# Four buffers for gathered rows in the routed experts of a decoder layer, and two steps moved

## The chip, the cores and the metric

The kernel runs on one core of a Trainium2 chip. The metric is the device time of one execution in microseconds, and the time of a kernel is the median over its runs.

## The reference

One decoder layer over 2048 tokens of width 1024, all in float32. A mixer (sliding window attention beside a gated recurrence) is followed by a layer norm; then comes a mixture of experts and a second layer norm. The change touches the mixture of experts and the end:

```python
h = _layernorm(ALPHA * h + mix, ln1_g[l], ln1_b[l])
# _moe: every token goes to 8 of 64 experts; the pairs are sorted by expert and cut into blocks of 128 rows
def body(acc, blk):
    toks, bw, e = blk                      # 128 token numbers, their weights, one expert
    xb = hp[toks]                          # gather
    yb = (jax.nn.silu(xb @ w_gate[e]) * (xb @ w_up[e])) @ w_down[e]
    return acc.at[toks].add(yb * bw[:, None]), None     # scatter with addition
...
shared = (jax.nn.silu(hf @ ws_gate) * (hf @ ws_up)) @ ws_down
h = _layernorm(ALPHA * h + acc + shared, ln2_g[l], ln2_b[l])
```

An expert has 1024 x 256 gate and up weights and 256 x 1024 down weights. In this input no expert has fewer than two blocks, as the order of the splits in the trace shows.

## The kernel before

The program has four stages, each a block in which every engine runs its own instruction stream: the mixer, the output projection with routing and placing, the routed experts (`experts`), and the shared expert of the last eight tiles with the second norm (`share_and_norm`).

**The split.** Float32 products are made on TensorE out of high and low parts. A raw tensor is copied to a high part by ScalarE (`ACT.Copy` into float32r), VectorE subtracts that from the raw one and gets the low part. So every weight and every activation costs a copy on ScalarE and a subtraction on VectorE. For an expert these are two halves of gate and up (`gu_hi`, `gu_lo`, split 0 and split 1) and the down weights (`d_hi`, `d_lo`, split 2).

**The experts' loop.** A turn is two steps (n = 0 and 1 in the code, with slot k = 0 and k = 1), one block of 128 rows each; the loop runs the number of turns that a table gives, here 81. A step of TensorE is: low part of gate and up for the next block, the down product `psY` of this block (12 matmuls), high part of gate and up for the block after, then the transposes of `H`. Slot 0's rows come as whole rows and TensorE transposes them (`psX`). Slot 1's rows come in four pieces and VectorE transposes them (`xF<-xg`, L2510 and L2512), in the step with k = 0.

**VectorE's step** in program order: `HT_lo` (L2589), the low part of the activations (`low_x`, L2518 or L2523), the row weights, `H` (L2565), with k = 0 the transposes of slot 1's rows (`turn_x`), split 0 of an expert whose first block is two blocks ahead, the copy of `psY`'s second half to `y` (L2602), split 1 of the same expert, and last split 2 (`d_lo`) if the next block is the first of its expert. TensorE's `psY` of the next step waits for `y`, and its fifth matmul for `HT_lo`. ScalarE makes `d_hi` at the end of the step before an expert's first block.

**GpSimd's step** in program order: wait for the index and the buffer, gather for the block four ahead (one indirect DMA for slot 0, four for slot 1), then wait for `y` and issue the scatter (L2406). There is one buffer for each slot's rows (`xg[0]`, `xg[1]`), so a gather can be asked for only when the transposes have read the block before.

**SyncE** loads the weights of the experts in order; the down weights of a buffer are loaded over when `dlo_s` says that split 2 has read them.

**The last stage.** SyncE issues the loads of the routed sums `acc` into `z`, in groups of three tiles (2g, 2g + 1 and 8 + g) for g below 4 and of one tile after that, with two loads of `hT_d` between, all without a wait. GpSimd adds the second sums to each tile by a DMA that adds (`add_second`, L2862), two groups ahead of the norm's arithmetic, which it issues behind them in the same stream. ScalarE's `squares(1)` waits for GpSimd's `mean(1)`, and TensorE's down product of the next tile waits for `high_HT`, which ScalarE has behind `squares`.

Of the kernel before, what the change touches and what calls it, by code (L numbers as in the profile page):

```python
# [6 lines left out]
P = 128  # L7
D = 1024
SEQ = 2048
TILES = SEQ // P  # L10
KC = D // P
# [21 lines left out]
QUADS = 4  # L33
# [10 lines left out]
AHEAD = 4  # L44
# [1628 lines left out]
def place_and_share(nc, ident, consts, place_in, mask, cum, dpf, dbf, table, n_turns, idx, pidx, tails_s, xg, gi, gi_s, x_in,  # L1673
# [10 lines left out]
    with ExitStack() as ctx:  # L1684
# [145 lines left out]
        @block.gpsimd  # L1830
        def _(pool):
            for k in range(2):
                pool.wait_ge(row_out[k], 32 * TILES // 2)
                pool.wait_ge(hT_out[k], 16 * TILES // 2)
                pool.wait_ge(kept_out[k], 16 * (TILES - EARLY) // 2)
            nc.gpsimd.memset(zeros[:], 0.0).then_inc(zeroed, 1)
            nc.clear_and_free_semaphores(spent)

            pool.wait_ge(pads_out, 48 + 16 * QUADS)
            for k in range(2):  # L1840
                pool.wait_ge(wt_out[k], 48 * TILES // 4)
            nc.gpsimd.memset(xg[1][:, :, PIECE:WIDE], 0.0).then_inc(tails_s, 1)
            pool.wait_ge(idx_s, 2)
            nc.gpsimd.tensor_copy(gi[0][:], idx[:, 0:1]).then_inc(gi_s, 1)
# [3 lines left out]
            nc.gpsimd.tensor_copy(gi[1][:], pidx[:, 0, :]).then_inc(gi_s, 1)  # L1848
            pool.wait_ge(gi_s, 2)
            gather_pieces(nc, hcut, xg[1], gi[1], x_in[1])  # L1850
# [348 lines left out]
def experts(nc, passed, w_gate, w_up, w_down, ident, htab, hcut, sums, table, n_turns, idx, pidx, tails_s, xg, gi, gi_s, x_in, acc_out, gu, guhi_s, gulo_s, wgu, wd, loaded, y, si, added,  # L2199
# [6 lines left out]
    with ExitStack() as ctx:  # L2206
# [21 lines left out]
        pairw = [sb(f"pairw{i}", [P, 1]) for i in range(2)]  # L2228
        psG = [ps(f"psG5_{i}", [P, 2 * FE]) for i in range(2)]
# [95 lines left out]
        def turns(eng, body):  # L2325

            nt = eng.value_load(n_turns[0:1, 0:1], min_val=0, max_val=BLOCKS // TURN)
            with eng.Fori(0, BLOCKS // TURN // BUNCH) as j:
                with eng.If(j * BUNCH < nt):
                    with eng.Fori(0, BUNCH) as q:  # L2330
                        i = j * BUNCH + q
                        with eng.If(i < nt):
                            body(i)
                        with eng.Else():
                            eng.sem_inc(passed, 1)
                with eng.Else():
                    eng.sem_inc(passed, 1)
            return nt
# [32 lines left out]
        def _(pool):  # L2371
            for k in range(2):
                if k == 0:
                    pool.wait_ge(turned[1], 1)
                    pool.wait_ge(pairw_s[0], 1)
                    nc.gpsimd.tensor_copy(gi[0][:], idx[:, 2:3]).then_inc(gi_s, 1)
                    pool.wait_ge(gi_s, 3)
                    gather_rows(nc, htab, xg[0], gi[0], x_in[0])
                else:
                    pool.wait_ge(odd_turned, 1)  # L2380
                    nc.gpsimd.tensor_copy(gi[1][:], pidx[:, 1, :]).then_inc(gi_s, 1)
                    pool.wait_ge(gi_s, 4)
                    gather_pieces(nc, hcut, xg[1], gi[1], x_in[1])
            nc.clear_and_free_semaphores(spent)
            for k in range(2):
                pool.wait_ge(acc_out[k], 16 * EARLY // 2)

            def body(i):
                for n, s, k in steps(i):


                    pool.wait_ge(next_gi_s, s.n + 1)
                    if k == 0:
                        pool.wait_ge(pairw_s[0], s.turn + 2)
                    carry_wait(pool, passed)
                    if k:
                        gather_pieces(nc, hcut, xg[1], gi[1], x_in[1])
                    else:
                        gather_rows(nc, htab, xg[0], gi[0], x_in[0])
                    s.wait(pool, si_s)  # L2400
                    for h in range(2):
# [5 lines left out]
                                                 in_=y[k][:], in_offset=None, compute_op=ALU.add).then_inc(added[k], 16)  # L2407

            nt = turns(pool, body)
            for k in range(2):  # L2410
                pool.wait_ge(x_in[k], (nt * (16 * TURN // 2) + 16 * AHEAD // 2) * (QUADS if k else 1))
# [3 lines left out]
        def _(act):  # L2415
# [11 lines left out]
            def gather_index(s, k):  # L2427
# [3 lines left out]
                if k:  # L2431
                    nc.scalar.activation(gi[1][:], pidx[:, bass.ds(s.turn + AHEAD // 2, 1), :].rearrange("p a g -> p (a g)"),
                                         ACT.Copy).then_inc(next_gi_s, 1)
                else:
                    nc.scalar.activation(gi[0][:], idx[:, bass.ds(s.n + AHEAD, 1)], ACT.Copy).then_inc(next_gi_s, 1)

# [48 lines left out]
            def body(i):  # L2485
                nexts = entries(act, i * TURN + 1, TURN + 1)
                for n, s, k in steps(i):
# [3 lines left out]
                    gather_index(s, k)  # L2491
# [10 lines left out]
        def _(dve):  # L2502
            def turn_x(nth):

                dve.wait_ge(x_in[1], nth * 16 * QUADS)
                if not (isinstance(nth, int) and nth == 1):
# [4 lines left out]
                                    xg[1][:, :, 0:FEATS].rearrange("p g (i c) -> p c g i", c=KC))  # L2511
                nc.vector.transpose(xF[:, KC, :].rearrange("p (g j) -> p g j", g=QUADS),  # L2512
                                    xg[1][:, :, FEATS:WIDE]).then_inc(odd_turned, 1)
# [33 lines left out]
            def pair_weight(entry, nth, slot):  # L2547
# [6 lines left out]
                dve.wait_ge(x_in[0], nth * 16)  # L2554
                carry_wait(dve, passed)
                nc.vector.tensor_copy(pairw[0][:], xg[0][:, bass.ds(entry.expert() + D, 1)]).then_inc(pairw_s[0], 1)
# [16 lines left out]
            pair_weight(block0, 1, 0)  # L2573
            dve.wait_ge(tails_s, 1)
            turn_x(1)
# [4 lines left out]
            when_first(dve, block0, lambda: split(block0, 2))  # L2580
# [3 lines left out]
            def body(i):  # L2584
                nexts = entries(dve, i * TURN + 1, TURN + 1)
                for n, s, k in steps(i):
# [6 lines left out]
                    if k == 0:  # L2593
                        pair_weight(nexts[n + 1], s.turn + 2, 0)
                        pair_weight(nexts[n], s.turn + 1, 1)
# [7 lines left out]
                    when_first(dve, nexts[n + 1], lambda: split(nexts[n + 1], 1))  # L2603
                    when_first(dve, nexts[n], lambda: split(nexts[n], 2))
# [4 lines left out]
        def _(pe):  # L2609

            def turn_x(nth):

                pe.wait_ge(x_in[0], nth * 16)
                carry_wait(pe, passed)
                rows = xg[0][:, 0:D].rearrange("p (q c) -> p c q", c=KC)
# [56 lines left out]
            turn_x(1)  # L2672
# [6 lines left out]
            turn_x(2)  # L2679

            def body(i):
                words = entries(pe, i * TURN, TURN + 2)
                for n, s, k in steps(i):
# [24 lines left out]
                    if k:  # L2708
                        turn_weights(s.turn + 2)
                        turn_x(s.turn + 3)  # L2710
# [12 lines left out]
def share_and_norm(nc, passed, ident, ln2_g, ln2_b, hT_d, acc, second, out, raw_gu, raw_d, shared_in, hT_in, n_turns, added):  # L2723
# [3 lines left out]
    with ExitStack() as ctx:  # L2727
# [90 lines left out]
        def _(sp):  # L2818
# [18 lines left out]
            for g in range(LATE):  # L2837
                for t in (2 * g, 2 * g + 1):
# [304 lines left out]
def decoder_layer(nc, x, w_in, conv_w, conv_b, w_rg, b_rg, w_ig, b_ig, lam, sinks, g_attn, g_lru, w_out,  # L3143
# [9 lines left out]
    with ExitStack() as ctx:  # L3153
# [77 lines left out]
        with ExitStack() as routing:  # L3231
# [26 lines left out]
            xg = [gathered.enter_context(nc.sbuf_tensor(f"xg{i}", shape, F, side="right"))  # L3258
                  for i, shape in enumerate(([P, ROW_W], [P, QUADS, WIDE]))]
            gi = [gathered.enter_context(nc.sbuf_tensor(f"gi{i}", [P, n], I32, side="right")) for i, n in enumerate((1, QUADS))]  # L3260
            pidx = gathered.enter_context(nc.sbuf_tensor("pidx", [P, WORDS // 2, QUADS], I32, side="right"))
            gathered.enter_context(nc.sbuf_tensor("gap_gu", [P, 8], F, side="right"))
            tails_s = gathered.enter_context(nc.semaphore("tails_s"))
            gi_s = gathered.enter_context(nc.semaphore("gi_s"))
            x_in = [gathered.enter_context(nc.semaphore(f"xg_in{i}")) for i in range(2)]
# [76 lines left out]
```

## Time and profile before

| | |
|---|---|
| median of 3 runs | 2506.89 us (2502.52 to 2510.63) |
| profiled execution, its own time | 2510.86 us |
| its span from the first to the last instruction | 2509.0 us |
| mean granted TensorE clock | 0.973 |
| TensorE busy | 2357.9 us (94%) |
| VectorE busy | 1758.6 us (70%) |
| ScalarE busy | 1179.1 us (47%) |
| GpSimd busy | 972.2 us (39%) |

The profiled execution's own time has 1.9 us around its span. The experts' loop lies between about 872 and 2386 us of the span, the last stage behind it. A busy engine is not an engine at its peak, and the idle time of an engine matters only where another one waits for it.

### The profile page before, as it was taken

The numbers are of one execution on the slowest core, as the hardware profiler recorded it, in microseconds if no ns is written. First come the engines' busy times: TensorE is split into PE (matmuls) and PEld (weight loads), VectorE is DVE, ScalarE is ACT, GpSimd is POOL, SyncE is SP. The second block draws the span as 40 slices with busy tenths as digits, with TensorE's granted clock in tenths as the row PEclk, the third lists the DMA queues.
The fourth block names the chain that finished last, engine by engine and source line by source line (L and its number), as shares of the span: only waits on it lengthen the run. The fifth ranks groups of instructions, "written<-read, shape, count | busy, mean of one in ns | idle before, by whom it ended". The sixth has DMA issues, their size and how long they took to land. (4 is left out here: it accounts for less than half of the span.)

```text
span 2509.0 us, 49346 instructions
## 1 busy us (share of the span) xinstructions
PE 2357.9 (94%) x11266; PEld 1904.2 (76%) x11268; DVE 1758.6 (70%) x2382; ACT 1179.1 (47%) x1863; POOL 972.2 (39%) x772
## 2 busy tenths in 40 slices
PE   8899999999998799999999999999999999999966
PEld 6576777678886677888778887787778888877855
DVE  6686767758878767667767677667766677767437
ACT  3525253532225545455554545545554546545334
POOL 0010100011110155554555555554655556555437
PEclk9999999979998899999999999999999999999988
DMA  6143434465655478878887878888888789887796
GB/s 252 76 168 122 137 116 141 136 222 196 216 206 208 167 240 269 248 220 271 254 269 232 260 232 247 272 261 257 255 241 249 226 240 300 274 247 229 180 248 202
DMA packets 165327, 551.13 MB, mean 220 GB/s; under 512 B 31344, under 2 KB 56080, under 8 KB 144784
## 3 DMA queue, kind: packets, MB, share of 16 engines
q1 hardware_dynamic: 109696, 355.03, 40.1%
q0 software_dynamic: 54960, 195.27, 31.0%
q8 instruction: 36, 0.59, 0.1%
q14 instruction: 27, 0.22, 0.0%
q10 hardware_dynamic: 608, 0.02, 0.0%
HBM read 394.99 MB, written 155.25 MB: 219 GB/s over the span
## 5 line engine op out<-in xcount | busy, mean ns | idle before, releaser
L2647 PE MATMUL psG<-gu_split,xT_hi 128*128 x2624 | 626.0, 391 | 3.4 <-ACT xT_hi L2421 1.9
L2647 PEld LDWEIGHTS psG<-gu_split,xT_hi 128*128 128x128 f32 x2624 | 494.9, 189 | 107.5 <-issue 4.1
L1669 POOL DMA_INDIRECT xg<-hcut,gi x332 | 376.6, 1134 | 144.0 <-issue 92.5
L2661 PE MATMUL psG<-gu_split,xT_lo 128*128 x1304 | 341.2, 403 | 0.0
L2526 DVE TENSOR_TENSOR gu_split<-raw_gu,gu_split (+1 forms) x127 | 289.4, 2279 | 69.2 <-ACT gu_split L2444 59.5
L2406 POOL DMA_INDIRECT acc<-y,si x81 | 170.4, 2104 | 413.1 <-DVE y L2602 376.5
L2661 PEld LDWEIGHTS psG<-gu_split,xT_lo 128*128 128x128 f32 x1304 | 233.1, 189 | 42.4
L2444 ACT ACTIVATE gu_split<-raw_gu x126 | 234.4, 1908 | 33.2 <-issue 16.6
L2510 DVE STREAM_TRANSPOSE xF<-xg 128x1024 f32<-128x1024 f32 x82 | 177.2, 2161 | 91.8 <-DMA xg<-hcut,gi 91.7
L2526 DVE TENSOR_TENSOR d_lo<-raw_d,d_hi (+1 forms) x64 | 146.6, 2291 | 123.9 <-ACT d_hi L2444 123.9
L2699 PE MATMUL psY<-d_hi,HT_lo 128*128 x648 | 204.3, 397 | 18.8 <-DVE HT_lo L2589 18.8
L2489 ACT ACTIVATE HT_hi<-psH 128x256 fp32r<-128x256 f32 x162 | 62.2, 384 | 335.0 <-PE psH L2668 335.0
L2699 PE MATMUL psY<-d_hi,HT_hi 128*128 x648 | 204.2, 396 | 16.2 <-DVE y L2602 11.6
L2406 POOL DMA_INDIRECT second<-y,si x81 | 193.9, 2394 | 35.6 <-issue 35.6
L2699 PE MATMUL psY<-d_lo,HT_hi 128*128 x648 | 200.8, 391 | 0.0
L2699 PEld LDWEIGHTS psY<-d_hi,HT_lo 128*128 128x128 f32 x648 | 119.2, 189 | 55.8 <-issue 33.1
L2699 PEld LDWEIGHTS psY<-d_hi,HT_hi 128*128 128x128 f32 x648 | 119.9, 188 | 51.8 <-issue 26.8
L2444 ACT ACTIVATE d_hi<-raw_d (+1 forms) x64 | 122.7, 1917 | 60.1 <-PE psY L2699 60.1
L2602 DVE COPY y<-psY 128x512 f32<-128x512 f32 x162 | 109.7, 677 | 51.6 <-PE psY L2699 51.6
L2699 PEld LDWEIGHTS psY<-d_lo,HT_hi 128*128 128x128 f32 x648 | 122.3, 189 | 26.6
L950 PE MATMUL psP<-xT_hi,wring 128*128 128x512 f32 x512 | 131.8, 407 | 11.2 <-ACT xT_hi L468 3.6
L418 POOL TENSOR_TENSOR OS<-QK 128x256 f32<-128x256 f32 x15 | 11.1, 739 | 317.6 <-ACT QK L560 317.6
(404 smaller groups left out, 4038.9 us busy)
## 6 DMA issues: line engine op xcount, KB each, us to landing
raw_gu<-in_w_gate_dram SPq DMA_DIRECT2D x64, 1024.0 KB, 5.2
raw_gu<-in_w_up_dram SPq DMA_DIRECT2D x64, 1024.0 KB
raw_d<-in_w_down_dram SPq DMA_DIRECT2D x64, 1024.0 KB
wring<-split_d SPq DMA_DIRECT2D x24, 1024.0 KB, 5.8
second<-blank SPq DMA_DIRECT2D x17, 512.0 KB, 6.8
split_d<-wring POOLq DMA_DIRECT2D x8, 1024.0 KB, 4.2
raw_d<-mixed SPq DMA_DIRECT2D x16, 512.0 KB, 5.3
xt<-in_x_dram SPq DMA_DIRECT2D x16, 512.0 KB, 5.7
```

The source lines that it names most:

```text
L418: nc.gpsimd.tensor_tensor(OS2[:], OSQ[:, 0:2, :], OSQ[:, 2:4, :], ALU.add).then_inc(os2_s, 1)
L950: m = nc.tensor.matmul(u.tile[:], w_[:, w, k, :], xT[x_][:, k, :], start=(n == 0), stop=(n == len(passes) - 1))
L1669: nc.gpsimd.indirect_dma_start(out=to[:, g, 0:PIECE], out_offset=None, in_=hcut.rearrange("r a w -> (r a) w"), in_offset=bass.IndirectOffs ...
L2406: nc.gpsimd.indirect_dma_start(out=sums[k], out_offset=bass.IndirectOffsetOnAxis(ap=si[k][:, 0:1], axis=0), in_=y[k][:], in_offset=None, c ...
L2444: nc.scalar.activation(dst, src, ACT.Copy).then_inc(done, 1)
L2489: nc.scalar.activation(HT_hi[:], psH[:, 0:FE].rearrange("p (a b) -> p a b", a=2), ACT.Copy).then_inc(HThi_s, 1)
L2510: nc.vector.transpose(xF[:, 0:KC, :].rearrange("p c (g j) -> p c g j", g=QUADS), xg[1][:, :, 0:FEATS].rearrange("p g (i c) -> p c g i", c=KC))
L2526: nc.vector.tensor_tensor(dst, src, hi, ALU.subtract).then_inc(dlo_s if n == 2 else gulo_s, 1)
L2602: nc.vector.tensor_copy(y[k][:, 512:], psY[:, 1, :]).then_inc(y_s[1], 1)
L2647: nc.tensor.matmul(psG[slot][:], xT_hi[slot][:, c, :], right[:, bass.ds(w, 1), c, :].rearrange("p a n -> p (a n)"), start=(n == 0 and c == ...
L2661: m = nc.tensor.matmul(psG[slot][:], xT_lo[slot][:, c, :], gu_hi[:, bass.ds(w, 1), c, :].rearrange("p a n -> p (a n)"), start=False, stop= ...
L2699: m = nc.tensor.matmul(psY[:, h, :], left[:, c, :], right[:, bass.ds(w, 1), c, h * 512:(h + 1) * 512].rearrange("p a n -> p (a n)"), start ...
```

## The change

- `xg` and `gi` get two buffers for each slot, `xg[k][side]`, and semaphores of their own. The loop's body is written out twice, for an even turn (side 0) and an odd turn (side 1), and the inner loop runs half as often. `AHEAD` goes from 4 to 6 blocks. Two more gathers stand ahead of the loop, with a second memset of the tail columns.
- GpSimd's step has the scatter first and the gather behind it.
- VectorE's split 2 leaves the end of the step before an expert's first block. It is made in the step of that first block, behind `turn_x` and ahead of split 0 and the copy of `y`.
- In the last stage SyncE waits, before the loads of group g (from 2 on), until the second sums of the last tile of group g - 2 have been added.
- A gap in the memory layout goes from 8 to 112 columns.

```diff
-AHEAD = 4
+AHEAD = 6
@@ turns
-                    with eng.Fori(0, BUNCH) as q:
-                        i = j * BUNCH + q
-                        with eng.If(i < nt):
-                            body(i)
-                        with eng.Else():
-                            eng.sem_inc(passed, 1)
+                    with eng.Fori(0, BUNCH // 2) as q:
+                        for side in range(2):
+                            i = j * BUNCH + q * 2 + side
+                            with eng.If(i < nt):
+                                body(i, side, j * (BUNCH // 2) + q)
+                            with eng.Else():
+                                eng.sem_inc(passed, 1)
@@ gpsimd, body
+                    s.wait(pool, si_s)
+                    for h in range(2):
+                        s.wait(pool, y_s[h])
+
+                    pool.wait_ge(added[k], s.turn * 16)
+                    carry_wait(pool, passed)
+                    nc.gpsimd.indirect_dma_start(out=sums[k], out_offset=..., in_=y[k][:], in_offset=None, compute_op=ALU.add).then_inc(added[k], 16)
                     pool.wait_ge(next_gi_s, s.n + 1)
                     if k == 0:
                         pool.wait_ge(pairw_s[0], s.turn + 2)
                     carry_wait(pool, passed)
+                    to = 1 - side
                     if k:
-                        gather_pieces(nc, hcut, xg[1], gi[1], x_in[1])
+                        gather_pieces(nc, hcut, xg[1][to], gi[1][to], x_in[1][to])
                     else:
-                        gather_rows(nc, htab, xg[0], gi[0], x_in[0])
-                    s.wait(pool, si_s)
-                    ...  (the wait for y and the scatter stood here)
@@ vector, ahead of the loop
             when_first(dve, block0, lambda: split(block0, 1))
-            when_first(dve, block0, lambda: split(block0, 2))
@@ vector, body
                     if k == 0:
-                        turn_x(s.turn + 2)
-                    when_first(dve, nexts[n + 1], lambda: split(nexts[n + 1], 0))
+                        turn_x(s.turn + 2, 1 - side, pair + 1 + side)
+                    when_first(dve, words[n], lambda: split(words[n], 2))
+                    when_first(dve, words[n + 2], lambda: split(words[n + 2], 0))
                     s.wait(dve, yps_s[1])
                     dve.wait_ge(added[k], s.turn * 16)
                     nc.vector.tensor_copy(y[k][:, 512:], psY[:, 1, :]).then_inc(y_s[1], 1)
-                    when_first(dve, nexts[n + 1], lambda: split(nexts[n + 1], 1))
-                    when_first(dve, nexts[n], lambda: split(nexts[n], 2))
+                    when_first(dve, words[n + 2], lambda: split(words[n + 2], 1))
@@ share_and_norm, sync
             for g in range(LATE):
+                if 2 <= g:
+                    sp.wait_ge(z_all[EARLY + g - 2], 16)
                 for t in (2 * g, 2 * g + 1):
                     if t < EARLY:
                         load_z(t)
```

Here `nexts` began one block later than `words` does, so `nexts[n]` is the same block as `words[n + 1]`.

## Rows read from the trace of the kernel before

**Rows 1.** Busy us: window, PE, PEld, DVE, ACT, POOL; PEclk, DMA share, GB/s.
```profile
872.00:2386.00 1514.00, 1476.99 (x6923) 1210.19 (x6924) 1052.15 (x1249) 765.63 (x1245) 818.49 (x573) 1.00 0.83 249
```
**Rows 2.** Waits of TensorE, 900 to 2380 us: total us, times, longest.
```profile
PE psY L2699 <- DVE HT_lo L2589: 18.8, 23, 0.9
PE psY L2699 <- DVE y L2602: 11.6, 13, 1.8
```
**Rows 3.** Busy time: twelve turns together, and two turns with late gathers.
```profile
1320.10:1534.30 214.20, 214.20 (x1017) 177.13 (x1017) 148.18 (x181) 107.53 (x181) 118.51 (x85) 1.00 0.83 243
1783.70:1824.70 41.00, 37.92 (x172) 30.29 (x172) 25.50 (x34) 17.77 (x30) 23.38 (x16) 0.96 0.92 265
```
**Rows 4.** Busy time in seven windows that hold 21 slow turns, their sum.
```profile
sum 420.10, PE 388.21 PEld 310.17 DVE 300.62 ACT 223.62 POOL 213.23; mean PE 55.46 PEld 44.31 DVE 42.95 ACT 31.95 POOL 30.46
```
**Rows 5.** Timeline of VectorE in one slow turn: start, us, idle before.
```profile
1239.50 2.29 DVE L2526 TENSOR_TENSOR d_lo<-raw_d,d_hi  x1 [2.44 <-ACT d_hi L2444]
...
1243.54 0.48 DVE L2565 SCALAR_TENSOR_TENSOR H<-psG,pairw,sg 128x256 f32<-128x256 f32 x1
1246.32 2.18 DVE L2510 STREAM_TRANSPOSE xF<-xg 128x1024 f32<-128x1024 f32 x1 [2.29 <-DMA xg<-hcut,gi]
...
1250.77 0.70 DVE L2602 COPY y<-psY 128x512 f32<-128x512 f32 x1
...
1253.56 0.44 DVE L2589 TENSOR_TENSOR HT_lo<-psH,HT_hi 128x256 fp32r<-128x256 f32 x1
```
**Rows 6.** Timeline of TensorE in the same turn.
```profile
1252.12 0.72 PE L2699 MATMUL psY<-d_hi,HT_hi 128*128 x2 [0.64 <-DVE y L2602]
...
1254.15 0.70 PE L2699 MATMUL psY<-d_hi,HT_lo 128*128 x2 [0.85 <-DVE HT_lo L2589]
```
**Rows 7.** A turn with splits 0 and 1 and no late gather: busy time.
```profile
1517.30:1535.30 18.00, 18.00 (x86) 14.73 (x85) 13.77 (x15) 10.66 (x16) 9.76 (x7) 1.00 0.66 189
```
**Rows 8.** Waits of VectorE, 900 to 2380 us.
```profile
DVE xF L2510 <- DMA xg<-hcut,gi: 89.6, 38, 5.7
DVE HT_lo L2589 <- ACT HT_hi L2489: 89.2, 36, 3.6
```
**Rows 9.** Timeline at the end of the loop: GpSimd's last two, TensorE's last matmul.
```profile
2384.88 0.95 POOL L1669 DMA_INDIRECT xg<-hcut,gi  x1 [0.30 <-issue]
2386.13 1.63 POOL L2406 DMA_INDIRECT second<-y,si  x1 [0.30 <-issue]
...
2393.15 0.79 PE L2713 MATMUL psG<-gu_split,xT_hi 128*128 128x512 f32 x1 [5.14 <-issue]
```
**Rows 10.** Timeline of the last stage on GpSimd.
```profile
2416.96 0.86 POOL L2862 DMA_DIRECT2D z<-second  x1 [3.19 <-DMA z<-acc]
...
2428.45 0.87 POOL L2862 DMA_DIRECT2D z<-second  x1 [2.98 <-DMA z<-acc]
2429.40 0.25 POOL L2894 TENSOR_SCALAR nmean<-total 128x1 f32<-128x1 f32 x1
...
2441.79 0.88 POOL L2862 DMA_DIRECT2D z<-second  x1 [1.01 <-DMA z<-acc]
```
**Rows 11.** Timeline of the last stage on VectorE and TensorE.
```profile
2416.96 1.22 DVE L3020 TENSOR_TENSOR z<-z,psY 128x1024 f32<-128x1024 f32 x1 [3.49 <-DMA z<-second]
...
2434.16 2.05 PE L3127 MATMUL psY<-s_d,HT_hi 128*128 128x512 f32 x4 [14.57 <-ACT HT_hi L2947]
```
**Rows 12.** DMA queues of the last stage: packets, MB, share of 16 engines.
```profile
q0 software_dynamic: 2784, 10.10, 41.0%
q1 hardware_dynamic: 4896, 17.83, 37.6%
```
**Rows 13.** All DMA queues that carried anything, 920 to 2380 us.
```profile
q0 software_dynamic: 49257, 170.73, 46.9%
q1 hardware_dynamic: 36525, 192.94, 36.6%
```
**Rows 14.** TensorE's first instruction in the experts' stage.
```profile
868.73 1.94 PE L2620 MATMUL psX<-ident,xg 128*128 128x128 f32 x8 [3.65 <-issue]
```

More of the change, by code:

```diff
@@ L2407, in body @@
                                                  in_=y[k][:], in_offset=None, compute_op=ALU.add).then_inc(added[k], 16)
+                    pool.wait_ge(next_gi_s, s.n + 1)
+                    if k == 0:
+                        pool.wait_ge(pairw_s[0], s.turn + 2)
+                    carry_wait(pool, passed)
+                    to = 1 - side
+                    if k:
+                        gather_pieces(nc, hcut, xg[1][to], gi[1][to], x_in[1][to])
+                    else:
+                        gather_rows(nc, htab, xg[0][to], gi[0][to], x_in[0][to])
             nt = turns(pool, body)
             for k in range(2):
-                pool.wait_ge(x_in[k], (nt * (16 * TURN // 2) + 16 * AHEAD // 2) * (QUADS if k else 1))
+                for side in range(2):
+                    pool.wait_ge(x_in[k][side], ((nt + AHEAD // TURN + 1 - side) >> 1) * 16 * (QUADS if k else 1))
             carry_wait(pool, passed)
@@ L2483, in _, with body @@
             when_first(act, block1, lambda: split_gate_up(block1, 1))
-            def body(i):
+            def body(i, side, pair):
                 nexts = entries(act, i * TURN + 1, TURN + 1)
@@ L2502, in _, with turn_x @@
         def _(dve):
-            def turn_x(nth):
-                dve.wait_ge(x_in[1], nth * 16 * QUADS)
+            def turn_x(nth, side, landed):
+                dve.wait_ge(x_in[1][side], landed * 16 * QUADS)
                 if not (isinstance(nth, int) and nth == 1):
@@ L2545, in split, with pair_weight @@
                 low(n, src, hi, lo)
-            def pair_weight(entry, nth, slot):
+            def pair_weight(entry, nth, slot, side=None):
                 if slot:
@@ L2572, in _ @@
                 dve.wait_ge(acc_out[k], 16 * EARLY // 2)
[L2573 to L2575 removed]
+            pair_weight(block0, 1, 0, 0)
+            dve.wait_ge(tails_s, 2)
+            turn_x(1, 0, 1)
             when_first(dve, block0, lambda: split(block0, 0))
@@ L2609, in _, with turn_x @@
         def _(pe):
-            def turn_x(nth):
-                pe.wait_ge(x_in[0], nth * 16)
+            def turn_x(nth, side, landed):
+                pe.wait_ge(x_in[0][side], landed * 16)
                 carry_wait(pe, passed)
-                rows = xg[0][:, 0:D].rearrange("p (q c) -> p c q", c=KC)
+                rows = xg[0][side][:, 0:D].rearrange("p (q c) -> p c q", c=KC)
                 for h in range(2):
@@ L2671, in _ @@
             block0, block1 = entries(pe, 0, 2)
-            turn_x(1)
+            turn_x(1, 0, 1)
             gate_up_high(1, 0, block0, 1)
@@ L2678, in _, with body @@
             turn_H(0)
-            turn_x(2)
-            def body(i):
+            turn_x(2, 1, 1)
+            def body(i, side, pair):
                 words = entries(pe, i * TURN, TURN + 2)
@@ L2709, in body @@
                         turn_weights(s.turn + 2)
-                        turn_x(s.turn + 3)
+                        turn_x(s.turn + 3, side, pair + 2)
             turns(pe, body)
```

72 lines of the change are left out of this document (34 added, 38 removed).

## The prediction, made before the changed kernel ran

> **What bounds the kernel now.** I read the busy time by stage first. The experts' loop has 1514 of the 2509 us, and TensorE is busy for 1476.99 of them, at the full granted clock [rows 1]. So the stage runs at TensorE's pace, and the change can only win back what TensorE loses there. The second view is what TensorE waits for: 18.8 us for VectorE's `HT_lo` and 11.6 us for VectorE's copy to `y` [rows 2]. Matmuls are pipelined and a short wait shows only in part, so the third view is the length of the turns, taken from the starts of the first `psY` matmul in the timeline. Twelve turns in a row without a stall take 214.2 us, 17.85 each, and TensorE is busy in all of it [rows 3]. Of the 80 turns that can be measured, 57 take 17.8 to 18.1 us, and 23 are longer. Of these, 21 have one and the same form and take 420.1 us together, 20.0 each [rows 4]. The other two follow each other and take 41.0 us [rows 3]. So stalls cost 21 x 2.15 + 5.3 = 50 us of the loop.
>
> The reader is to see what the 21 have in common. In VectorE's timeline of one of them `turn_x` starts 2.29 us late, because slot 1's gathered rows have not landed; split 0, the copy to `y`, split 1 and `HT_lo` stand behind it in that order [rows 5]. TensorE then waits 0.64 us for `y` and 0.85 us for `HT_lo` [rows 6]. All 21 have splits 0 and 1 in the step with k = 0 and a gather that is over 2 us late. A turn with these splits and no late gather takes 18.0 us [rows 7]. With a late gather and no such splits a turn takes 17.85, so nearly half of the 38 waits for the gather [rows 8] cost nothing. The length of a turn with these splits is about 17.6 us plus the wait for the gather: 19.67 us with the shortest, 2.04 us, and 20.65 with 3.07 us, in the same timelines.
>
> **The buffers and the order on GpSimd.** A second buffer for each slot lets the gather be asked for a whole turn, 17.85 us, earlier. The longest wait is 5.7 us [rows 8], so all of them go. GpSimd's work is the same; the scatter of slot 1 no longer stands behind four issues of 0.95 + 0.30 us [rows 9], and the gathers, now behind the scatter, have a turn to spare. I cost the new order at nothing; if that spare turn were gone, the cost would be the waits that are there now.
>
> **Split 2, a step later.** This is where the gain goes. For an expert whose first block is at slot 0, `d_lo` stood at the end of the step before, one with k = 1. VectorE did it there in idle time: it had waited 2.44 us for `d_hi` ahead of it [rows 5]. After the change the same subtraction stands in the step with k = 0, behind `turn_x` and ahead of split 0 and `y`, if this block is the first of its expert. Splits 0 and 1 stand there if the block two ahead is a first one. Both hold exactly for an expert of two blocks that begins at slot 0. The timeline shows `d_lo` at the end of the step before in all 21 slow turns: they are these experts. In the 15 turns with splits 0 and 1 and no late gather there was no `d_lo` in the step before. So in every one of the 21 the wait for the gather is taken out, and a subtraction of 2.29 us is put in its place. `H` can't come earlier to make up for it, since it follows at once on the silu that waits for TensorE. Instructions that follow each other without a wait overlap by about 0.08 us (`turn_x` begins 0.08 us before `H` ends in turns without a late gather), so the subtraction counts as a wait of 2.29 - 0.16 = 2.13 us. A slow turn becomes 17.6 + 2.13 = 19.7 us: 21 x (20.0 - 19.7) = 6 us, of which I take 5, as these waits may be shorter in other executions. Where the first block is at slot 1, `d_lo` moves to a step without `turn_x`: three subtractions and the copy are 3 x 2.2 + 0.6 = 7.2 us against the 9.4 us of such a step, and the idle time of up to 3.6 us that VectorE has ahead of `HT_lo` [rows 8] covers the rest. If that cover were gone, each of some ten such turns would be 1 to 2 us longer.
>
> The two other long turns had gathers 2.94 and 5.68 us late, with `d_lo` at the end of a step with k = 0. Both causes go: 41.0 - 2 x 17.85 = 5.3 us. But the profiled execution takes 2510.86 us, 4.0 above the median, and such an accident may be in it alone. I count 5 us against the profiled execution and 2 against the median.
>
> SyncE asks for the next down weights up to 7 us later, since `dlo_s` comes later, and for nothing else: gate and up of the next expert wait for splits that come behind. The weights are used two experts on; hidden.
>
> **The loop written twice.** The skipped turns behind the last one are 5.14 us of issue on TensorE [rows 9]; half as many back edges may save up to 1 us. I take nothing. At the end GpSimd's scatter comes first and the four pieces last: `y` is ready near 2384, so their issue ends at 2384 + 1.6 + 4 x 1.25 = 2391 us. They landed some 6 us behind the last issue in the slow turn [rows 5], with full queues; here I estimate 2 to 6. The stage then ends between 2393 and 2397, against 2393.9, the end of TensorE's last matmul [rows 9]: 0 to 3 us, of which I take 1.
>
> **Loads in groups.** `z<-acc` lands and `z<-second` is issued every 3.85 us: three times from 2416.96 to 2428.45 [rows 10]. The two queues share the engines by halves; the shares of this stage give 46 us for 34 half megabytes on the one, 1.4 each, and 50 us for 19 on the adding one, 2.6 each [rows 12]. Now the ninth load lands at 2428.45, GpSimd's mean stands behind it at 2429.40 [rows 10], ScalarE's squares behind that, and TensorE waits 14.57 us until 2434.16 [rows 11]. After the change the loads of group 2 are asked for when the third tile's second sums are in, at 2416.96 [rows 11], just when the sixth load has landed. The loading queue runs empty for some 2.5 us, the additions get ahead by one, and that costs the ninth load 2.6 us. Nothing wins it back: the twelfth load (2441.79) waits behind the same bytes, and the norm behind it runs at its own pace. From below 0, if the engines lose nothing; from above 4 us, if the next handover does it again. I take 3. The output's stores are issued later too, behind the last load, but the last store waits for the last tile as before.
>
> **The sum** against the profiled execution: -5 (slow turns), -5 (late gathers), +1 (end of the loop), +3 (loads), -6 in all: 2504.9. Against the median, with -2 for the second term: 2506.9 - 3 = 2503.9. In proportion to the profiled execution it would be 2500.9; I take 2502.
>
> **The rivals.** (1) The slow turns go altogether, since VectorE finds 2.1 us elsewhere. They would then take the 18.0 us of the turn without the wait [rows 7]: 21 x 2.0 = 42, and with 2 for the late gathers and 4 for the ends 2506.9 - 42 - 2 + 4 = 2467. For it: the subtraction leaves the end of the step before. Against it: VectorE was idle there [rows 5], and `H` waits for TensorE.
> (2) The loads in groups cost more than the loop gives back. Where a handover leaves both queues dry, each of the two that matter (groups 2 and 3) costs a pair of 3.85 us, and with 3 for the loop's end that is 11: 2506.9 + 11 - 4 = 2514. It decides from 7 us on. For it: the first handover falls on an empty queue [rows 11]; against it: additions are in flight at each.
> (3) The doubled body no longer stays in an engine's instruction memory. In the loop before only the two data queues carried anything [rows 13], so no instructions were fetched. Where TensorE enters new code it stands for 3.65 us [rows 14]; at 40 back edges that is 146 us, 2650. On VectorE the 3.6 us ahead of `HT_lo` [rows 8] would hide it. The Trainium skill (Runtime: NRT & Kernel Launch, Instruction fetch mechanics) says that a taken branch out of the window that an engine holds costs a fetch before execution goes on. The trace agrees so far that a body of one turn stays in; no run here shows two.
> (4) The gathers are as late as before, because contention and not the request sets their landing. Then slow turns have the wait and the subtraction: 21 x 2.1 = 44, 2551. Against it: no wait was over 5.7 us [rows 8], and a turn is three times that.
>
> **How the numbers follow.** A measurement of this kernel tells 0.3%, 7.5 us, from no change: faster is below 2499.4, slower above 2514.4. The forecast (2495 to 2509) has 0.6: 0.2 of it below 2499.4, 0.4 within. Rival 1 has 0.1, faster. Rival 2 (2508 to 2518) has 0.15: 0.06 within, 0.09 slower. Rival 3 has 0.06, slower. Rival 4 and mishaps not named have 0.09: 0.02 faster, 0.01 within, 0.06 slower. Faster 0.32, same 0.47, slower 0.21. The range leaves out rival 1, rival 3 and the far part of the rest: 2490 to 2514.
>
> **What the changed profile would show.** Right: VectorE's wait for the gather falls from 89.6 us to under 5; in the same 21 turns its order is `turn_x`, `d_lo`, split 0, `y`, split 1, `HT_lo` without a gap; TensorE's waits for `y` and `HT_lo` stay above 20 us together, and these turns take 19.6 to 19.8. The ninth addition of the last stage lies 2 to 4 us later behind the stage's start, and TensorE's long wait with it. Wrong: turns of 18.1 us where three splits meet (rival 1), instruction fetches in the loop (rival 3), or a last stage that gets shorter.

## The result: slower, and where the time went

| | before | after |
|---|---|---|
| median us | 2506.25 (2502.52 to 2510.63) | 2544.47 (2539.73 to 2547.38) |
| profiled execution, its span | 2510.86, 2509.0 | 2547.38, 2545.6 |

The ratio is 1.015, with a 95% interval of 1.0127 to 1.0173: 38 us or 1.5% slower, where 2502 with a range of 2490 to 2514 was predicted. The page of the changed kernel, its first lines:

```profile
span 2545.6 us, 49175 instructions
...
PE 2359.9 (93%) x11267; PEld 1896.9 (75%) x11268; DVE 1764.9 (69%) x2382; ACT 1178.2 (46%) x1863; POOL 891.5 (35%) x780
```

The busy time of the experts' loop answers to [rows 1] (columns as there):

```profile
885.00:2413.00 1528.00, 1462.58 (x6838) 1190.46 (x6838) 1043.01 (x1233) 754.12 (x1232) 716.46 (x563) 1.00 0.82 243
```

TensorE now stands for 65 us of its loop, against 37 in [rows 1]. I number the steps from 0, two to a turn. The 80 turns between the first `psY` matmul of step 0 and that of step 160 take 1520.0 us, against 1482.2 in the kernel before: 37.8 us more, where the two spans differ by 36.6. TensorE's waits in the loop answer to [rows 2] and VectorE's to [rows 8]; ScalarE's row has no counterpart before (total us, times, longest; "remote" means that the profile names no instruction that ended the wait):

```profile
PE psY L2705 <- DVE HT_lo L2595: 22.8, 35, 0.9
PE psY L2705 <- DVE y L2609: 18.6, 21, 1.4
PE psY L2705 <- ACT HT_hi L2496: 17.0, 20, 1.2
...
DVE HT_lo L2595 <- ACT HT_hi L2496: 270.6, 89, 5.5
...
ACT HT_hi L2496 <- remote: 87.8, 25, 3.8
```

VectorE has no wait for a gather any more (89.6 us in [rows 8]). New is that TensorE waits for `HT_hi`, and that ScalarE starts `HT_hi` late without a releaser in the trace. One such place, in the timelines of GpSimd, TensorE and ScalarE (start, us, instruction, idle before):

```profile
1916.70 0.99 POOL L1669 DMA_INDIRECT xg<-hcut,gi  x1 [0.30 <-issue]
1917.99 0.95 POOL L1669 DMA_INDIRECT xg<-hcut,gi  x1 [0.30 <-issue]
1919.25 0.95 POOL L1669 DMA_INDIRECT xg<-hcut,gi  x1 [0.30 <-issue]
1920.50 0.95 POOL L1669 DMA_INDIRECT xg<-hcut,gi  x1 [0.30 <-issue]
1921.76 1.63 POOL L2403 DMA_INDIRECT acc<-y,si  x1 [0.30 <-issue]
1923.69 0.99 POOL L1662 DMA_INDIRECT xg<-htab,gi  x1 [0.30 <-issue]
...
1921.75 0.38 PE L2674 MATMUL psH<-ident,H 128*128 128x128 f32 x2
1921.89 2.09 PE L2667 MATMUL psG<-gu_split,xT_lo 128*128 x8
1924.48 0.72 PE L2705 MATMUL psY<-d_hi,HT_hi 128*128 x2 [0.50 <-ACT HT_hi L2496]
...
1918.79 1.92 ACT L2451 ACTIVATE d_hi<-raw_d  x1 [0.91 <-PE psY L2705]
1923.80 0.38 ACT L2496 ACTIVATE HT_hi<-psH 128x256 fp32r<-128x256 f32 x1 [3.09 <-remote]
```

The same step in the kernel before:

```profile
1906.90 0.39 PE L2668 MATMUL psH<-ident,H 128*128 128x128 f32 x2
...
1907.32 0.38 ACT L2489 ACTIVATE HT_hi<-psH 128x256 fp32r<-128x256 f32 x1 [1.46 <-PE psH L2668]
```

ScalarE is free from 1920.71 on and needs only `psH`. Before, `HT_hi` starts 0.42 us behind the start of the pair of `psH` matmuls; now it starts 2.05 us behind it, while TensorE goes on with its eight `psG` matmuls at the usual pace. I counted such late starts (over 0.3 us behind the usual distance, where ScalarE was idle) from 928 to 2300 us of each trace: 0 of 148 in the kernel before, 24 of 145 in the changed one, 49 us together. Expectations below count over the whole loop, so they have some more (26 for 24, 49 for 44). The signal is late, and not ScalarE: the trace keeps the times of the semaphore updates, and the one that `HT_hi` waits for comes 1.92 us behind the start of the second `psH` matmul here, against 0.28 us in the kernel before, with `HT_hi` 0.02 us behind it in both. By the Trainium skill (Perfetto Trace Analysis, Tensor Engine Instruction) the profiled start of a matmul is the start of its reads, its end is an estimate, and the signal goes out when PSUM has acknowledged the last write. The trace agrees so far that the update is 1.6 us later than usual while TensorE's rows show nothing late.

`HT_hi` is only the easiest of these signals to count. Where ScalarE waits for the last `psG` matmul to start `sg`, it starts late by the same measure in 27 of 137 cases (35 us together, 6 of them in the 21 turns of the prediction) against 0 of 146 before. So TensorE's completions fall behind in stretches, not one signal by itself, and the count of `HT_hi` is a marker of that, not the whole of the loss.

### The profile page after: what moved, and what is told of

Read it like the earlier page. It is cut to its first block and busy times, and to the rows that moved or that the text cites. A ratio compares the mean times of both kernels' runs of the same rounds, so it can differ in the third digit from the quotient of the medians.

```text
span 2545.6 us, 49175 instructions
## 1 busy us (share of the span) xinstructions
PE 2359.9 (93%) x11267; PEld 1896.9 (75%) x11268; DVE 1764.9 (69%) x2382; ACT 1178.2 (46%) x1863; POOL 891.5 (35%) x780
## 5 line engine op out<-in xcount | busy, mean ns | idle before, releaser
L1669 POOL DMA_INDIRECT xg<-hcut,gi x336 | 327.4, 974 | 102.3 <-issue 101.1
L2595 DVE TENSOR_TENSOR HT_lo<-psH,HT_hi 128x256 fp32r<-128x256 f32 x162 | 68.6, 424 | 306.1 <-ACT HT_hi L2496 279.5
L2403 POOL DMA_INDIRECT second<-y,si x81 | 159.2, 1965 | 339.0 <-DVE y L2609 176.3
```

The lines of the kernel that those rows point to most:

```text
L1669: nc.gpsimd.indirect_dma_start(out=to[:, g, 0:PIECE], out_offset=None, in_=hcut.rearrange("r a w -> (r a) w"), in_offset=bass.IndirectOffs ...
L2403: nc.gpsimd.indirect_dma_start(out=sums[k], out_offset=bass.IndirectOffsetOnAxis(ap=si[k][:, 0:1], axis=0), in_=y[k][:], in_offset=None, c ...
L2595: nc.vector.tensor_tensor(HT_lo[:], psH[:, 0:FE].rearrange("p (a b) -> p a b", a=2), HT_hi[:], ALU.subtract).then_inc(HTlo_s, 1)
```

## The experiments

Kernels in one table were run together on one chip, beside the kernel before (in the last table `h` on one chip and `i` on another). The last column is what the 80 turns say: the mean of the 21 turns of the prediction, the mean of the 59 others, and the late starts of `HT_hi`. In the kernel before these are 20.00, 18.00 and 0; in the changed one 20.21, 18.57 and 24.

**Undoing the parts.** `e1_order` puts GpSimd's gather ahead of its scatter again, `e2_dlo` puts split 2 back to the end of the step before, `e3_both` does both, `e4_all_but_late` takes the groups out of the last stage's loads as well. The diffs are against the changed kernel where nothing else is said.

```diff
 # e1_order, e3_both, e4
-                    s.wait(pool, si_s)
...  (the wait for y and the scatter)
                     pool.wait_ge(next_gi_s, s.n + 1)
...
                         gather_rows(nc, htab, xg[0][to], gi[0][to], x_in[0][to])
+                    s.wait(pool, si_s)
...  (the wait for y and the scatter)
 # e2_dlo, e3_both, e4
-                    when_first(dve, words[n], lambda: split(words[n], 2))
                     when_first(dve, words[n + 2], lambda: split(words[n + 2], 0))
...
                     when_first(dve, words[n + 2], lambda: split(words[n + 2], 1))
+                    when_first(dve, words[n + 1], lambda: split(words[n + 1], 2))
 # e4
-                if 2 <= g:
-                    sp.wait_ge(z_all[EARLY + g - 2], 16)
```

> The changed kernel with one thing put back: in each step GpSimd asks for the gather first and scatters behind it. Theory A (the scatter-first order lets GpSimd issue six or seven indirect transfers without a pause, and TensorE's signal to ScalarE is held up behind them): the late starts of HT_hi (26, 52.9 us together) and of sg go, the 21 two-block turns stay at 19.9 us since the low part of the down weights still stands there, and the time is that of the kernel before, 2506 us (2498 to 2514). Rival B (the doubled loop body, the second buffers or asking six ahead hold the signal up): no change from the changed kernel, 2544 us. Rival C (the new place of the low part shifts the step so that the signal meets the gathers): 2544 us too.

> The changed kernel with one thing put back: the low part of the down weights is subtracted at the end of the step before. Theory A: the 21 slow turns go from 19.9 to about 18.1 us, 38 us less, and the late signals stay: 2506 us (2500 to 2515). Rival B: the same here. Rival C (its place causes the late signals too): both go, 2467 us (2460 to 2475).

> Both put back (gather ahead of scatter, low part at the end of the step before); the second buffers, six ahead, the doubled body and the grouped loads stay. Theory A: neither the late signals nor the slow turns: 2467 us (2460 to 2475), with no turn of 19.9 us. Rival B: the slow turns go but the late signals stay: 2506 us. Rival C: 2467 us, as theory A.

> As the kernel with both put back, and the late blocks' loads of the last stage issued at once again instead of in groups of three. If the grouping costs the 3 us that were forecast for it, this is 3 us faster than the kernel with both put back; if it costs nothing, as the trace of the changed kernel reads (ninth add 33.8 us and twelfth 47.0 us behind the start of the stage in both), the two agree within 1 us.

| | us | ratio to before (95%) | 21 turns, 59 turns, late |
|---|---|---|---|
| e1_order | 2542.75 | 1.0104 (1.0076 to 1.0133) | 21.56, 18.01, 33 |
| e2_dlo | 2502.28 | 0.9963 (0.9943 to 0.9982) | 18.06, 18.51, 26 |
| e3_both | 2491.23 | 0.9911 (0.9893 to 0.9928) | 19.25, 18.03, 44 |
| e4_all_but_late | 2490.78 | 0.9915 (0.9895 to 0.9936) | as e3, 44 |

My theory A fell (2506 us forecast for `e1_order`), and so did rival C (2467 for `e2_dlo`). Rival B comes nearest, with 2544, 2506 and 2506 forecast for the first three, but its third is 15 us too high. Gather first does not take the late signals away, it moves them. With scatter first no late start of `HT_hi` falls into the 21 turns, and the 59 others are long (18.5 for 18.0). With gather first 21 of the 44 in `e3_both` and 19 of the 33 in `e1_order` fall into the 21 turns, and most of the lost time is there; ScalarE's reads of `psX` are late as well there (38 of 63 in `e3_both`), and `sg` is not. With split 2 back in its place the 21 turns are 18.06 us (`e2_dlo`), 2.15 us less than in the changed kernel, so the moved subtraction does cost about what the prediction said; but even `e3_both`, without either, has 44 late starts, 78 us together, of which part shows. The groups of loads cost nothing that can be measured: `e3_both` and `e4_all_but_late` agree within 0.5 us.

**One part alone on the kernel before, and what brings the late signals.** `b1_dlo_only` moves split 2 in the kernel before. `f1_double` writes its loop body out twice. `f4_shift` and `f5_light` are `e3_both` with other places for the new buffers, and with less weight traffic: `f5_light` loads only the first eighth of the gate and up weights and computes with stale values in the rest.

```diff
 # f1_double, on the kernel before
-                    with eng.Fori(0, BUNCH) as q:
-                        i = j * BUNCH + q
+                    with eng.Fori(0, BUNCH // 2) as q:
+                        for side in range(2):
+                            i = j * BUNCH + q * 2 + side
 # f4_shift
+        xg1_1 = sb("xg1_1", [P, QUADS, WIDE])
+        sb("gap_x", [P, 256])
-        xg = [[xg[0][0], sb("xg0_1", [P, ROW_W])], [xg[1][0], sb("xg1_1", [P, QUADS, WIDE])]]
+        xg = [[xg[0][0], sb("xg0_1", [P, ROW_W])], [xg[1][0], xg1_1]]
 # f5_light
+                        part = dst.shape[1] // (1 if sm is down_in else 8)
-                        sp.dma_start(dst, w[0, bass.ds(e, 1)].rearrange(rows, p=P)).then_inc(sm, 16)
+                        sp.dma_start(dst[:, 0:part], w[0, bass.ds(e, 1)].rearrange(rows, p=P)[:, 0:part]).then_inc(sm, 16)
```

> The kernel before with the low part of the down weights subtracted a step later, and nothing else. Theory D (the new place by itself costs the 40 us by which the changed kernel and the one with this part put back differ): 2545 us or more (2540 to 2560), since the 21 two-block turns also keep their wait for gathered rows. Rival E (the new place is harmful only with six blocks ahead and two buffers, where it meets a gather at the step's start): no more than 10 us above the kernel before.

> The kernel before with its loop body written out twice (two turns a pass), and nothing else: the same instructions, buffers and four blocks ahead. Late signals from TensorE (HT_hi more than 0.3 us behind its usual 0.31 us after psH) are 0 of 162 in the kernel before and 49 in the kernel with both parts put back, at what looks like the same schedule. If the doubled body brings them, this one has 20 or more and takes 2520 to 2545 us; if the second buffers do, it has none and takes as long as the kernel before.

> The kernel with both parts put back, its two new buffers in the opposite order in SBUF and 1 KB per partition apart. If the late signals come from where the gathered rows land (the address), their count of 49 and the time of 2491 us change by more than 5 us; if not, both stay.

> The kernel with both parts put back, but gate and up weights loaded only in their first eighth (1 MB less 7 eighths each; the rest of the arithmetic runs on stale weights, so the output is not the reference's). If the late signals need the weight loads' traffic beside the gathers, they go (fewer than 5 of 162) and the time is about 2460 us (80 turns of 17.95 us, 1436, for 1468 in the loop); if they come from the gathers and scatters alone, 40 or more stay and the time is within 5 us of 2491 us.

| | us | ratio to before (95%) | 21 turns, 59 turns, late |
|---|---|---|---|
| b1_dlo_only | 2646.74 | 1.057 (1.0542 to 1.0598) | 22.26, 19.67, 0 |
| f1_double | 2504.53 | 1.0 (0.9989 to 1.0011) | 19.89, 18.01, 0 |
| f4_shift | 2459.88 | 0.9822 (0.9802 to 0.9842) | 18.07, 17.91, 0 |
| f5_light | 2465.95 (one run) | | 18.07, 17.91, 0 |

On this chip the doubled body is free and brings no late signal. `b1_dlo_only` missed theory D by 102 us and rival E by more. Its waits:

```profile
PE psY L2698 <- DVE y L2602: 105.0, 54, 3.2
...
DVE xF L2510 <- DMA xg<-hcut,gi: 239.6, 74, 6.6
```

TensorE waits 105 us for `y`, against 11.6 in [rows 2], and VectorE 240 us for gathers, against 89.6 in [rows 8]. I read this as a loop that feeds its own delay: with one buffer the subtraction delays `y`, `y` delays GpSimd's scatter, the next turn's four pieces stand behind that scatter, and land later still. The order of the instructions allows it and the two waits fit it; no run takes it apart. In the changed kernel the second buffers are there.

`f4_shift` is the surprise: it has no late signals, and TensorE has no idle time left in the loop. Its busy time:

```profile
928.00:2328.00 1400.00, 1400.00 (x6629) 1156.36 (x6629) 1004.49 (x1196) 733.66 (x1195) 784.22 (x547) 1.00 0.86 258
```

And that with a pattern of issues on GpSimd and SyncE which is the same within 0.05 us in the place compared here (step 17), first in `e3_both`, then in `f4_shift`:

```profile
1044.28 1.00 POOL L1669 DMA_INDIRECT xg<-hcut,gi  x1 [0.30 <-issue]
...
1048.10 0.95 POOL L1669 DMA_INDIRECT xg<-hcut,gi  x1 [0.30 <-issue]
1049.35 2.68 POOL L2412 DMA_INDIRECT second<-y,si  x1 [0.30 <-issue]
...
1048.54 0.38 PE L2675 MATMUL psH<-ident,H 128*128 128x128 f32 x2
...
1050.75 0.38 ACT L2496 ACTIVATE HT_hi<-psH 128x256 fp32r<-128x256 f32 x1 [3.26 <-remote]
...
1042.92 0.34 SPq L2361 DMA_DIRECT2D raw_gu<-in_w_gate_dram  x1
```

```profile
1037.31 1.00 POOL L1669 DMA_INDIRECT xg<-hcut,gi  x1 [0.30 <-issue]
...
1041.11 0.95 POOL L1669 DMA_INDIRECT xg<-hcut,gi  x1 [0.31 <-issue]
1042.36 2.70 POOL L2414 DMA_INDIRECT second<-y,si  x1 [0.30 <-issue]
...
1041.59 0.38 PE L2677 MATMUL psH<-ident,H 128*128 128x128 f32 x2
...
1042.00 0.39 ACT L2498 ACTIVATE HT_hi<-psH 128x256 fp32r<-128x256 f32 x1 [1.48 <-PE psH L2677]
...
1035.95 0.34 SPq L2363 DMA_DIRECT2D raw_gu<-in_w_gate_dram  x1
```

The gate load is issued 5.6 us ahead of `psH` in both, the fourth piece 0.4 to 0.5 us ahead of it and the scatter 0.8 us behind it; `HT_hi` follows 2.21 us behind `psH` in the one and 0.41 in the other. So the issues alone do not make the signal late. The other traces say the same: all 24 late starts of the changed kernel lie in chains of seven indirect transfers on GpSimd with under 1 us between them, of which the window holds 24; but the kernel before has 49 such chains, and `g2_dlo_shift` below 25, without a late start.

**The changed kernel with its buffers moved.** `g1_after_shift` is the changed kernel with the buffers of `f4_shift`, `g2_dlo_shift` the same with split 2 back, `g3_swap` and `g4_gap` are `e3_both` with only the order of the two buffers or only the gap of 1 KB.

> The changed kernel as it is, but its two new buffers in the opposite order in SBUF and 1 KB per partition apart, as in the kernel whose late signals went. Theory F (the changed kernel lost its 38 us to late signals from TensorE that hang on where its second buffers lie, and otherwise did what was forecast: 21 turns of 19.9 us, the rest at 17.85 to 18.1): no late signals in the loop and 2499 us (2494 to 2506), 45 us less than the changed kernel. Rival G (the late signals of the changed kernel come from its order on GpSimd or the new place of the low part, whatever the address): 2535 us or more.

> The same with the low part of the down weights back at the end of the step before, GpSimd still scattering first. It differs from the 2460 us kernel (both put back, buffers moved) in GpSimd's order alone. Forecast of the prediction, that the order costs nothing: 2460 us (2455 to 2465), no turn above 18.3 us. If scattering first makes signals late by itself: 2475 us or more, with late signals counted.

> The kernel with both parts put back (2491 us, 49 late signals), its new buffers in the opposite order and without the gap between them: the four-piece buffer at 135840, the row buffer at 140448. If the place of the four-piece buffer decides: 2460 us and no late signals, as in the kernel with the gap. If that of the row buffer decides (its start is 1 KB lower than there): 2491 us.

> The same with the old order and the gap alone: the row buffer at 135840 as in the 2491 us kernel, the four-piece buffer 1 KB higher, at 141216 for 140192. If the four-piece buffer must lie at 135840: 2491 us and late signals; if any place other than 140192 does: 2460 us.

| | us | ratio to before (95%) | 21 turns, 59 turns, late |
|---|---|---|---|
| g1_after_shift | 2499.03 | 0.9978 (0.9966 to 0.999) | 19.67, 17.92, 0 |
| g2_dlo_shift | 2465.77 | 0.9842 (0.9824 to 0.9861) | 18.07, 17.93, 0 |
| g3_swap | 2463.27 | 0.9836 (0.9816 to 0.9856) | 18.07, 17.91, 0 |
| g4_gap | 2459.89 | 0.9823 (0.9803 to 0.9842) | 18.07, 17.91, 0 |

`g1_after_shift` is the prediction as it was meant: 2499 us. One of its 21 turns in VectorE's timeline, and below it TensorE's, answer to [rows 5] and [rows 6]:

```profile
1255.44 2.21 DVE L2519 STREAM_TRANSPOSE xF<-xg 128x1024 f32<-128x1024 f32 x1
...
1257.73 2.29 DVE L2535 TENSOR_TENSOR d_lo<-raw_d,d_hi  x1
1259.90 2.31 DVE L2535 TENSOR_TENSOR gu_split<-raw_gu,gu_split  x1
1262.10 0.72 DVE L2611 COPY y<-psY 128x512 f32<-128x512 f32 x1
1262.70 2.31 DVE L2535 TENSOR_TENSOR gu_split<-raw_gu,gu_split  x1
1264.90 0.45 DVE L2597 TENSOR_TENSOR HT_lo<-psH,HT_hi 128x256 fp32r<-128x256 f32 x1
...
1263.47 0.73 PE L2707 MATMUL psY<-d_hi,HT_hi 128*128 x2 [0.46 <-issue]
...
1265.49 0.70 PE L2707 MATMUL psY<-d_hi,HT_lo 128*128 x2 [0.84 <-DVE HT_lo L2597]
```

The subtraction stands where the wait for the gather stood, VectorE has no gap from `turn_x` to `HT_lo`, and TensorE stands idle for 0.46 and 0.84 us where it did for 0.64 and 0.85 in [rows 6]. Putting it back to the end of the step before (`g2_dlo_shift`) is worth 33 us on the same chip: 21 x (19.67 - 18.07) = 34.

**How small a shift, and is it the place?** `h1_gap64`, `h2_gap256` and `h3_gap512` are `e3_both` with gaps of 64, 256 and 512 bytes between the row buffer (135840 to 140192) and the four-piece buffer; `h4_alone` leaves the four-piece buffer at 140192 and puts the row buffer behind it. `i1_both_again` and `i2_after_again` repeat `e3_both` and the changed kernel.

> The kernel with both parts put back (2491 us), its four-piece buffer 64 bytes higher (140256 for 140192). If the lateness hangs on a coincidence of bytes or lines with what the weight loads or TensorE touch: 2460 us already here; if it hangs on a region of some KB: 2491 us.

> The same, 256 bytes higher (140448). The run with 1 KB took 2460 us; where between 0 and 1 KB the change lies tells the grain: 2491 or 2460 us, nothing between.

> The same, 512 bytes higher (140704): 2491 or 2460 us, as above.

> The kernel with both parts put back, its four-piece buffer at the old 140192 behind an empty stretch, and the row buffer behind it at 144800. If the four-piece buffer's own place decides: 2491 us with 40 or more late signals; if it takes both where they were: 2460 us.

> The kernel with both parts put back once more, unchanged in every byte, to tell the place of its buffers from the chip that it ran on. If the place decides: 2491 us with 49 late signals, as before. If the chip does: about 2460 us and none, or something else again.

> The changed kernel once more, unchanged. If the place of its buffers decides: 2544 us with 26 late signals. If the chip does: about 2499 us, as the kernel with moved buffers, whose 21 slow turns are all that is left.

| | us | ratio to before (95%) | late |
|---|---|---|---|
| h1_gap64 | 2463.19 | 0.9832 (0.9804 to 0.9861) | 0 |
| h2_gap256 | 2459.79 | 0.9819 (0.979 to 0.9847) | 0 |
| h3_gap512 | 2459.92 | 0.9819 (0.9791 to 0.9848) | 0 |
| h4_alone | 2459.58 | 0.9818 (0.9774 to 0.9862) | 0 |
| i1_both_again | 2490.98 | 0.9911 (0.9892 to 0.993) | 45 |
| i2_after_again | 2555.88 | 1.0176 (1.0155 to 1.0196) | 24 |

All nine kernels with moved buffers have no late start at all, of `HT_hi`, `sg` or the reads of `psX`; all seven profiles of kernels with the buffers as the change has them and full weight loads have 24 to 45. The late starts repeat: `i2_after_again` has them in the same 24 steps as the changed kernel. But read the condition closely. The four-piece buffer's own place is harmless (`h4_alone`), the row buffer's too (`h1_gap64`), and 64 bytes are enough, which is odd for an effect of place. The new buffers take the gathers of every second turn only, and the late starts do not follow that: 11 and 13 of the changed kernel's, 20 and 24 of `e3_both`'s, lie in even and odd turns.

And the chips are a rival. Kernels `e` ran on one chip and `i` on another, both unmoved; `f`, `g` and `h` ran on three more, where every full kernel with the second buffers was a moved one. Which chip the changed kernel ran on first is not on record. The kernel before itself takes 2513 and 2512 us on the chips of `e` and `i`, against 2504 to 2505 on the three others, and 2506 beside the first runs of the changed kernel; of `e` and `i` no trace of it was kept. A property of the chips would divide the results in the same way. The expectation of `i1_both_again` took a repetition on another chip for the test; it is weaker than one with a moved kernel beside it. `f5_light`, unmoved, ran on the chip of `f4_shift`, so its lack of late signals (2465.95 us, at 181 GB/s of DMA traffic against 255 in `e3_both`) may come from the lighter traffic or from the chip. In the same way `f1_double` shows only that the doubled body is free on a chip on which no late signal was ever seen.

## Why the prediction was wrong, step by step

- **What bounds the kernel: right.** The loop is TensorE's, and the change won or lost only stalls. The floor of the turns was right as well: without any stall they are 17.9 to 18.07 us (`f4_shift`).
- **The failed step: "I cost the new order at nothing", for the buffers and the order on GpSimd.** The waits for gathers went, all of them, as said. But the sum has no term for TensorE's signals coming late, and this term is 49 us: the loops of the changed kernel and of `g1_after_shift` take 1520.0 and 1470.6 us. That the late `HT_hi` starts also add up to 49 us is chance, since other signals are late and part of each delay is hidden. No rival named the term either. Without late signals the kernel takes 2499.03 us, within the range. The order itself is close to nothing in the loop: `f4_shift` and `g2_dlo_shift` take 1436.2 and 1437.1 us there.
- **Split 2: right.** The same 21 turns, the order without a gap, 19.67 us without late signals for 19.7 forecast (20.21 with them). That is 7 us less than before for the 21 turns, where 6 were forecast.
- **Rival 1** asked how fast these turns would be with neither wait nor subtraction: 18.07 us in `f4_shift` and 2460 us for the kernel, where the prediction said 18.0 and 2467. In the changed kernel it did not come true; VectorE found no time elsewhere.
- **The two accidental turns: right.** They take 35.7 us together in `g1_after_shift`, for 41.0 before: the 5.3 us that were counted. In the changed kernel they take 38.2.
- **The end of the loop: 1 us forecast, 3.2 measured.** From step 161's first `psY` to the last stage's first instruction it is 14.4 us before and 17.6 after. It is 15.1 to 15.3 in `e1_order`, `e3_both`, `e4_all_but_late` and `f4_shift`, where the gather comes first, and 17.5 to 17.6 in `e2_dlo`, `g1_after_shift` and `g2_dlo_shift`: 2.4 us come with the scatter first, that is with four pieces issued last.
- **Loads in groups: 3 us forecast, nothing measured.** The first handover leaves the loading queue dry, as said, but the time of the next loads is not lost. GpSimd's timeline of the last stage, to be set against [rows 10]:

```profile
2431.00 0.94 POOL L2860 DMA_DIRECT2D gain<-in_ln_g_dram  x1 [6.49 <-POOLq L2206]
...
2453.78 0.88 POOL L2870 DMA_DIRECT2D z<-second  x1 [3.54 <-DMA z<-acc]
2460.95 0.88 POOL L2870 DMA_DIRECT2D z<-second  x1 [6.30 <-DMA z<-acc]
2463.53 0.87 POOL L2870 DMA_DIRECT2D z<-second  x1 [1.71 <-DMA z<-acc]
2464.78 0.87 POOL L2870 DMA_DIRECT2D z<-second  x1 [0.38 <-DMA z<-acc]
2465.73 0.25 POOL L2902 TENSOR_SCALAR nmean<-total 128x1 f32<-128x1 f32 x1
```

  These additions are issued when the tile's load has landed. The seventh comes 7.17 us behind the sixth, 3.3 more than the steady 3.85; the eighth and ninth follow it at 2.58 and 1.25 us, and the ninth lies 33.78 us behind the stage's first instruction, against 33.75 before. The step "nothing wins it back" was wrong: loads that had been asked for together landed in a burst. `e4_all_but_late` agrees with `e3_both` within 0.5 us. That the two ends came to 3.4 us together, for 4 forecast, is luck: one term was 2.2 too small and the other 3 too large.
- **Rivals 3 and 4: wrong.** No instruction was fetched in the loop, and no gather came late. Rival 4's 2551 us lies near the result by coincidence.

What stays open is what makes TensorE's signals late. Shown is that they are late, and that kernels which differ in the place of two buffers, and perhaps in the chip, take 2544 us with them and 2499 without, and their variants 2491 and 2460 (the loops 1520.0 and 1470.6, 1468.0 and 1436.2). Split 2's place and GpSimd's order are not needed for them and do not cure them, as `e3_both` and `e2_dlo` have them. Not separated are the places of the two new buffers and the chip; nor, if it is the chip, which of the second buffers, six blocks ahead and the doubled body brings them out there.

## What to carry to other kernels

Where a wait is taken away, look at what is put in its place. Here the second buffers, with split 2 left where VectorE was idle and no late signals, win 39 us on one chip (`g2_dlo_shift`, 2466 against 2505), and the moved subtraction takes 33 of them back (`g1_after_shift`). A new buffer may come with more than the waits that it removes, so count late signals (the time from a matmul's start to its reader's, with the reader idle) in both traces before believing a sum of durations; and run kernels that differ by placement beside each other on one chip, or the chip stays a rival. A load that is asked for later cost nothing here, since the loads behind it landed in a burst.

## What was not expected of the hardware

- TensorE's signal to ScalarE, 0.31 us behind the start of the second `psH` matmul in 148 of 148 cases before, came up to 3.0 us late in other kernels, while TensorE's own rows kept their pace. In all but 2 of the 240 cases GpSimd was in a chain of five to seven indirect transfers with under 1 us between them. The kernel before and `f4_shift` have such chains and no late signal, so they are a company, not a cause that is shown.
- A subtraction of 2.29 us moved by one step cost 141 us with one buffer for each slot (`b1_dlo_only`), and 33 us with two (`g1_after_shift` against `g2_dlo_shift`).
- Plain loads of 512 KB landed 2.6 and 1.25 us apart after a gap, against 3.85 us in the steady stream. The additions to the same tiles kept landing 3.8 us apart.
